# The attention sink of the windowed heads, as a column of the score tile

## What is computed

```
s_band = jnp.einsum('bnqhgd,bnkhd->bnhgqk', qb, kb).astype(F32) * scale
s_band = jnp.where(valid[None, :, None, None], s_band, -jnp.inf)
s_ctx = jnp.einsum('bnqhgd,bphd->bnhgqp', qb, k_ctx).astype(F32) * scale
s_sink = jnp.broadcast_to(sink.astype(F32).reshape(1, 1, Hk, G, 1, 1), s_band.shape[:-1] + (1,))
p = jax.nn.softmax(jnp.concatenate([s_band, s_ctx, s_sink], axis=-1), axis=-1)
p_band = p[..., :3 * BAND_BLOCK].astype(v.dtype)
p_ctx = p[..., 3 * BAND_BLOCK:3 * BAND_BLOCK + P].astype(v.dtype)
o = jnp.einsum('bnhgqk,bnkhd->bnqhgd', p_band, vb) + jnp.einsum('bnhgqp,bphd->bnqhgd', p_ctx, v_ctx)
```

## Time and profile before

| what | value |
|---|---|
| time, median of 3 runs | 1140.9 us (1140.78 to 1141.33) |
| the profiled execution | 1138.51 us, of which the span is 1136.7 us |
| TensorE busy | 1068.4 us, 94% of the span |
| VectorE busy | 416.9 us, 37% |
| ScalarE busy | 396.4 us, 35% |
| GpSimd busy | 538.1 us, 47% |
| mean granted TensorE clock | 0.979 of full |

### The profile page before, as it was taken

The page is one execution under the profiler, slowest core; times in us unless marked ns, Lnnn a source line. Parts: engine busy times, 40 slices in busy tenths (PEclk is TensorE's granted clock), DMA queues, the critical chain, the costliest instruction groups (busy, mean ns, idle before and its releaser), DMA issues.

```text
span 1136.7 us, 16312 instructions
## 1 busy us (share of the span) xinstructions
PE 1068.4 (94%) x6725; PEld 972.0 (86%) x6725; DVE 416.9 (37%) x850; ACT 396.4 (35%) x630; POOL 538.1 (47%) x422
## 2 busy tenths in 40 slices
PE   4799999997999999999999898789989999999997
PEld 3598899886989999999999696645879999999996
DVE  3757889157651111111112404286471111111222
ACT  0532332356343332232223423476334332332221
POOL 0364548541735555555557141230254566565662
PEclk9899999999989999999999998989989999999998
DMA  8633444546655666646668531620052454534441
GB/s 309 227 114 130 149 166 149 157 163 248 182 160 178 199 191 198 198 144 191 200 200 211 158 112 27 154 74 2 3 147 75 118 142 112 142 96 135 118 123 56
DMA packets 202053, 166.40 MB, mean 146 GB/s; under 512 B 20269, under 2 KB 184188, under 8 KB 201852
## 3 DMA queue, kind: packets, MB, share of 16 engines
q1 hardware_dynamic: 189280, 135.74, 40.2%
q10 hardware_dynamic: 12700, 29.63, 7.5%
HBM read 162.43 MB, written 2.92 MB: 145 GB/s over the span
## 4 chain that ended last, share of the span: by engine, by line
PE 83%; DVE 6%; ACT 3%; DMA 3%; POOL 2%; issue 1%; ACTq 0%; SPq 0%; DVEq 0%
PE banks L455 22%; PE banks L456 21%; PE banks L457 21%; PE banks L549 3%; PE banks L526 2%; PE banks L528 2%; PE banks L527 2%; POOL w_lo L1119 2%; PE banks L693 2%; DMA raw<-in_ada_w 2%; DVE ht L1621 1%; DVE h_lo L1612 1%; PE banks L542 1%; DMA xtok<-in_x_sample 1%; PE banks L990 1%
## 5 line engine op out<-in xcount | busy, mean ns | idle before, releaser
L1119 POOL TENSOR_TENSOR w_lo<-raw,w_hi 128x512 fp32r<-128x512 f32 (+2 forms) x398 | 512.7, 1319 | 581.4 <-ACT w_hi L1143 581.4
L455 PE MATMUL banks<-h_hi,w_hi 128*128 128x384 f32 (+1 forms) x1040 | 352.1, 339 | 6.0 <-DVE h_lo L1612 3.5
L457 PE MATMUL banks<-h_hi,w_lo 128*128 128x384 f32 (+1 forms) x1040 | 348.5, 335 | 0.0
L456 PE MATMUL banks<-h_lo,w_hi 128*128 128x384 f32 (+1 forms) x1040 | 348.4, 335 | 0.0
L1143 ACT ACTIVATE w_hi<-raw 128x2048 fp32r<-128x2048 f32 (+4 forms) x112 | 187.9, 1678 | 244.7 <-PE banks L457 135.8
L455 PEld LDWEIGHTS banks<-h_hi,w_hi 128*128 128x128 f32 (+1 forms) x1040 | 194.9, 187 | 16.0 <-issue 13.5
L456 PEld LDWEIGHTS banks<-h_lo,w_hi 128*128 128x128 f32 (+1 forms) x1040 | 195.1, 188 | 0.6
L457 PEld LDWEIGHTS banks<-h_hi,w_lo 128*128 128x128 f32 (+1 forms) x1040 | 195.0, 187 | 0.6
L1675 DVE TENSOR_TENSOR uf<-sa,banks 128x384 f32<-128x384 f32 x44 | 24.4, 554 | 325.1 <-PE banks L457 318.9
L455 PE MATMUL banks<-u_hi,w_hi 128*128 128x384 f32 x352 | 119.4, 339 | 0.0
L457 PE MATMUL banks<-u_hi,w_lo 128*128 128x384 f32 x352 | 118.2, 336 | 0.0
(11 more groups left out here) (324 smaller groups left out, 1184.3 us busy)
## 6 DMA issues: line engine op xcount, KB each, us to landing
raw<-in_ffn_w SPq DMA_DIRECT2D x88, 512.0 KB, 5.2
raw<-in_ada_w SPq DMA_DIRECT2D x28, 1024.0 KB, 6.3
raw<-in_ffn_w SPq DMA_DIRECT2D x32, 704.0 KB, 4.6
vada_raw<-in_ada_w ACTq DMA_DIRECT2D x20, 1024.0 KB, 6.5
raw<-in_w_in_even SPq DMA_DIRECT2D x18, 1024.0 KB, 5.3
raw<-in_w_out_even SPq DMA_DIRECT2D x4, 1024.0 KB, 6.2
raw<-in_w_in_odd SPq DMA_DIRECT2D x3, 1024.0 KB, 9.4
raw<-in_w_in_odd SPq DMA_DIRECT2D x8, 256.0 KB, 4.2
```

The lines of the kernel that those rows point to most:

```text
L455: pe.matmul(out, s_hi, m_hi, start=first and j == 0, stop=False)
L456: pe.matmul(out, s_hi, m_lo, start=False, stop=False)
L457: mm = pe.matmul(out, s_lo, m_hi, start=False, stop=last and j == len(terms) - 1)
L1119: ins = pool.tensor_tensor(low_part(s)[:, at:to], raw[u % RAW][:, at:to], high(s)[:, at:to].bitcast(F32), ALU.subtract)
```

## The change

The sink becomes one more key. `sink_score` holds sink times 8 (the inverse of the scale) on all partitions. `scores` writes it into a column behind each head's keys, with a matmul of the identity (stationary) and one column of `sink_score` (moving), in fp32. Maximum, exponential and row sum then run over 129 or 385 columns and take the sink in by themselves; the small steps L2022, L2024, L2035 and L1528 go, and sliding jobs take the one multiplication that low-rank jobs have. The scaling of the probabilities and the transposes leave the sink's column out. Because a head's probabilities take 385 columns, the halves of `pr` lie 386 apart instead of 384, and some tiles of the odd layer are laid out in another order, so that the larger `pr` finds room.

```diff
-        neg_sink = sb("neg_sink", [P, 8])
+        sink_score = sb("sink_score", [P, 8])
...
+        def width(job):
+            return job[5] + (job[0] == "swa")
...
                     for i, j in enumerate(pairs):
                         for x in range(2):
-                            mm = pe.matmul(both[:, 512 * x + i * nk:512 * x + i * nk + nk],
-                                           qc[64 * x:64 * x + 64, j, tq], kT[64 * x:64 * x + 64, k0:k0 + nk],
-                                           start=i == 0, stop=t == 0, skip_group_check=True)
+                            pe.matmul(both[:, 512 * x + i * wide:512 * x + i * wide + nk],
+                                      qc[64 * x:64 * x + 64, j, tq], kT[64 * x:64 * x + 64, k0:k0 + nk],
+                                      start=i == 0, stop=t == 0, skip_group_check=True)
+                    for i, j in enumerate(pairs):
+                        for x in range(2):
+                            at = 512 * x + i * wide + nk
+                            mm = pe.matmul(both[:, at:at + 1], ident, sink_score[:, 4 * x + j:4 * x + j + 1],
+                                           start=False, stop=True, skip_group_check=True)
...
-                            e = act.activation(pr_[:, 384 * x + i * nk:384 * x + (i + 1) * nk],
-                                               both[:, 512 * x + i * nk:512 * x + (i + 1) * nk], ACT.Exp,
+                            e = act.activation(pr_[:, SIDE * x + i * wide:SIDE * x + (i + 1) * wide],
+                                               both[:, 512 * x + i * wide:512 * x + (i + 1) * wide], ACT.Exp,
                                                scale=scale, bias=s_[:, 1, c:c + 1], accum_out=s_[:, 2, c:c + 1])
-                    if kind == "swa":
-                        e = act.activation(s_[:, 3, 0:nh], s_[:, 3, 0:nh], ACT.Exp)
...
-            step(dve.tensor_scalar(neg_sink[:, :], rowb[:, 0:8], -1.0, None, ALU.mult))
+            step(dve.tensor_scalar(sink_score[:, :], rowb[:, 0:8], 64 ** 0.5, None, ALU.mult))
...
-                    step(dve.tensor_reduce(two(0), sides(both[:, :], np_ * nk).rearrange("p x (i k) -> p x i k", i=np_),
+                    step(dve.tensor_reduce(two(0), sides(both[:, :], np_ * width(jobs[n])).rearrange("p x (i k) -> p x i k", i=np_),
                                            AX.X, ALU.max))
-                    if kind == "swa":
-                        step(dve.scalar_tensor_tensor(two(1), two(0), -scale, sinks(neg_sink[:, :], pairs),
-                                                      ALU.mult, ALU.min))
-                        dve.tensor_tensor(two(3), sinks(rowb[:, 0:8], pairs), two(1), ALU.add)\
-                            .then_inc(S["neg_max"], 1)
-                    else:
-                        dve.tensor_scalar(s_[:, 1, 0:nh], s_[:, 0, 0:nh], -scale, None, ALU.mult)\
-                            .then_inc(S["neg_max"], 1)
+                    dve.tensor_scalar(s_[:, 1, 0:nh], s_[:, 0, 0:nh], -scale, None, ALU.mult).then_inc(S["neg_max"], 1)
...
-                    if kind == "swa":
-                        step(dve.tensor_tensor(s_[:, 2, 0:nh], s_[:, 2, 0:nh], s_[:, 3, 0:nh], ALU.add))
                     step(dve.reciprocal(s_[:, 4, 0:nh], s_[:, 2, 0:nh]))
```

More of the change, by code:

```diff
@@ L132, in ada_units @@
     raise KeyError(place)
+SIDE = 386
 SEAM_UNITS = (("up0", 0), ("in1", 0), ("up1", 0))
@@ L252, in build @@
         PF, SI = PFSI[:, 0], PFSI[:, 1]
-        (const_odd, qc, kT, vt, cqf, ckvf, cq_hi, cq_lo, ckv_hi, ckv_lo, kr4, qn, qr, kn, vm, krr, rt, pr, pT,
-         cin_k, cin_c, cin_r, ident_r, band_r, out_k, out_c, out_r, st) = overlay([
-            ("const_odd", [P, NALL - NCONST], F32), ("qc", [P, 4, T], F32), ("kT", [P, TK], F32), ("vt", [P, 4, P], F32), ("cqf", [P, 3, T], F32),
+        (const_odd, ident_r, band_r, qc, kT, vt, cqf, ckvf, cq_hi, cq_lo, ckv_hi, ckv_lo, kr4, qn, qr, kn, vm, krr, rt,
+         cin_k, cin_c, cin_r, out_k, out_c, out_r, st, pT, pr) = overlay([
+            ("const_odd", [P, NALL - NCONST], F32), ("ident_r", [P, P], BF16), ("band_r", [P, 2, P], BF16),
+            ("qc", [P, 4, T], F32), ("kT", [P, TK], F32), ("vt", [P, 4, P], F32), ("cqf", [P, 3, T], F32),
             ("ckvf", [P, 2, T], F32), ("cq_hi", [P, 3, T], F32R), ("cq_lo", [P, 3, T], F32R),
@@ L259, in build @@
             ("qn", [P, 4, T], F32), ("qr", [P, 2, T], F32), ("kn", [P, 4, TK], F32), ("vm", [P, 4, 512], F32),
-            ("krr", [P, T], F32), ("rt", [P, 2, TL], F32), ("pr", [P, PR, 768], F32), ("pT", [P, 2, 768], F32),
+            ("krr", [P, T], F32), ("rt", [P, 2, TL], F32),
             ("cin_k", [P, P], F32), ("cin_c", [P, 256], F32), ("cin_r", [P, 4, 32], F32),
-            ("ident_r", [P, P], BF16), ("band_r", [P, 2, P], BF16),
-            ("out_k", [P, P], F32), ("out_c", [P, 256], F32), ("out_r", [P, 32], F32), ("st", [P, PR, 5, 4], F32)])
+            ("out_k", [P, P], F32), ("out_c", [P, 256], F32), ("out_r", [P, 32], F32), ("st", [P, PR, 5, 4], F32),
+            ("pT", [P, 2, 768], F32), ("pr", [P, PR, 2 * SIDE], F32)])
         _, x_hi, x_lo = overlay([("below", [P, 22848], F32), ("x_hi", [P, 2048], F32R), ("x_lo", [P, 2048], F32R)])
@@ L424, in sides @@
             return ap.rearrange("p (x n) -> p x n", x=2)[:, :, 0:w]
-        def sinks(ap, pairs):
-            return ap.rearrange("p (x j) -> p x j", x=2)[:, :, pairs[0]:pairs[-1] + 1]
+        def width(job):
+            return job[5] + (job[0] == "swa")
         vada_at_up = {f + 1: n // 4 for f, n in VADA_AT_UP.items() if n % 4 == 3}
@@ L949, in scores @@
                     pe.wait_ge(S["masks_ready"], 1)
-                both = score.fill(pe, ("s", n))
+                both, wide = score.fill(pe, ("s", n)), width(job)
                 tq = slice(t * P, (t + 1) * P)
@@ L985, in turned @@
                 both = turned_in.fill(pe, ("pT", n))
-                w = len(pairs) * nk
                 for x in range(2):
-                    for i in range(w // P):
-                        at = 384 * x + i * P
-                        tr = pe.transpose(both[:, 512 * x + i * P:512 * x + i * P + P], pr[:, n % PR, at:at + P], ident)
+                    for i in range(len(pairs)):
+                        for k in range(0, nk, P):
+                            at = SIDE * x + i * width(job) + k
+                            to = 512 * x + i * nk + k
+                            tr = pe.transpose(both[:, to:to + P], pr[:, n % PR, at:at + P], ident)
                 tr.then_inc(turned_in.done, 1)
@@ L1515, in _ @@
                     scale = 64 ** -0.5 if kind == "swa" else 96 ** -0.5
-                    s_, pr_, nh = st[:, n % PR], pr[:, n % PR], 2 * len(pairs)
+                    s_, pr_, wide = st[:, n % PR], pr[:, n % PR], width(jobs[n])
                     act.wait_ge(S["neg_max"], n + 1)
@@ L2039, in _ @@
                             c = x * np_ + i
-                            p = pr[:, (n - 1) % PR, 384 * x + i * nk:384 * x + (i + 1) * nk]
+                            at = SIDE * x + i * width(jobs[n - 1])
+                            p = pr[:, (n - 1) % PR, at:at + nk]
                             ins = dve.tensor_scalar(p, p, s_[:, 4, c:c + 1], None, ALU.mult)
```

## The result

The changed kernel takes 1143.3 us (median of 10 runs, 1140.85 to 1146.52), the kernel before, run beside it, 1140.2 us (10 runs, 1137.94 to 1142.05): a ratio of 1.0028 (95% interval 1.0017 to 1.004), 3.1 us slower. That lies in the range, near its upper end, and beyond the 0.2% up to which "the same" reached. The changed kernel's runs fall into two fives, 1140.9 to 1142.9 us at a mean granted clock of 0.976 or 0.977 and 1143.7 to 1146.5 us at one of 0.969 to 0.973, and the profiled execution (1141.55 us, span 1139.0, clock 0.976) is one of the first, so its trace shows less than the median loss.

What follows compares the result with a forecast made beforehand. The prediction took the sliding heads' stage as a ring of waits over TensorE, VectorE and ScalarE, its changes passed on one for one; +0.6+0.5-1.5+0.5 = +0.1 us on the 1140.9 median gave 1141.0 us, range 1138.3 to 1143.8.

Steps and rivals of the forecast that it cites:

- The first term: Start of the sliding heads' stage: job 0's sink instructions +0.89, removed VectorE step -0.19 and exponential -0.10, net +0.6 us.
- The second term: Half-clock stretch, about 738 to 744.5: eight sink instructions of jobs 2 and 3 cost 1.6, partly given back, +0.5 us.
- run there in half the time: Half-clock stretch: 2.2 us of work pushed past the clock's rise takes half as long there, 1.1 behind in all.
- The third term: GpSimd's two weight-split windows, 744.6 to 758.5: one caught VectorE step fewer in each, -1.5 us (ends -2.4 and +0.2).
- both scalings behind them were caught: GpSimd's windows: the normalising after the exponential is held up in both, giving back 2x1.3, so +0.2 us for this part.
- The fourth term: Steady part, four jobs: TensorE becomes the bound, turns of 3.19 against 3.05 us, +0.14x4, taken as +0.5 us.
- A: Ahead of job 2's scores: TensorE's gap shrinks to about 1.1 us, the clock does not fall; 1138.5 us, chance 0.17.
- B: Same stretch: a TensorE break before 744.5 prolongs half clock; 1144.3 us at worst, 1143.2 with one job hit, chance 0.18.
- in that stretch TensorE has a backlog: Half-clock stretch: argument against a break in TensorE's work before 744.5 that would keep the clock from rising.
- C: Sink instructions throughout the stage are nearly free, by the skill's issue-gap rule of about 25 ns; -2.2 us, 1138.7, chance 0.05.

## Why the prediction was off, step by step

**The first term held.** Fill: +0.6 forecast, +0.71 in the trace.

**The second term failed: the half-clock stretch, forecast at +0.5 us.** The price of a sink instruction in it was right (0.20 taken, 0.22 measured). Wrong was the step "run there in half the time", which kept the clock's return at 744.5, where it stood in the trace of before. It moved to 749.41, so nothing was given back. At job 4's start, where this part ends (744.69 before, 748.19 now), the changed kernel was 2.31 us behind, 0.71 of it from the fill: 1.6 us for this part, all of the 8x0.20, near the upper end of 1.7. A clock read from one execution was taken as fixed, while the change altered the very work ahead of it and under it.

**The third term's size held, by luck in part.** From job 4 to job 7 the changed kernel needs 11.39 us for 13.12: -1.7, where the sum had -1.5. One caught step took the place of two, as described, but both scalings behind them were caught, and that case the sum had priced at +0.2. The -1.7 is made of two larger numbers. Job 4's turn took 1.57 us more, with its scores at half clock and four sink instructions for which the sum has no term (the lag at job 5's start is 3.88). From job 5 to job 7 the changed kernel needs 6.85 us for 10.15, 3.3 less. The second half-clock stretch of the kernel before lay there (its value matmuls took 1.55 us for 0.88, job 6's scores 1.58 for 0.92); it is gone, and so is most of TensorE's waiting for VectorE. I read part of the 3.3 as no gain of the change by itself: TensorE, late by the half clock, lost time in which it had waited for VectorE before. The kernel with the steps off, which has no sinks and no such lag, wins 1.65 us from job 5 to job 7 (8.50 for 10.15), half of it. What is due to the steps and what to the missing half clock no run tells apart. In this execution the 3.3 give back what job 4 had lost and the second term, and the stage ends only 1.2 us late.

**The fourth term held in size, for another reason.** From job 7 to the low-rank heads it is 9.89 us for 9.30, +0.6 where +0.5 was forecast. TensorE became the bound, as forecast, but with turns of 2.99 us where 3.19 was taken and 3.05 stood before: -0.06 a turn, not +0.14 (four times 0.14 is 0.56, which the sum took as 0.5). What makes the part longer is its first turn, 3.92 us (759.58 to 763.50): GpSimd's second window now ends at 761.62 instead of 758.49 and reaches into it. The 2.74 for TensorE's turn without idle time was too much; without the sinks it is 2.53.

**The rivals.** A had the idle time right (1.1 forecast, 0.97 measured), but the clock fell all the same. B is what happened to that stretch; its own test (0.50 at 746) came out. Its reason did not: it asked for a break in TensorE's work before 744.5, and none opened after 739.91. Its price for one job hit, 1143.2, is within 0.1 us of the median measured, which is luck in part: the kernel before ran at 1140.2 beside it and not at 1140.9, so as a difference it is +2.3 against +3.1. The argument against it, "in that stretch TensorE has a backlog", was no protection. 0.18 was too little for it: no row of before showed one-column work at half clock, and the clock row of one execution was all that spoke for an early return. C fell for fp32: 0.12 us, not 0.025. For bf16 instructions the rule in the Trainium skill, "TensorE: Matmul & The Clock Gate", section "Back-to-back issue gap", holds (0.03 measured), so the sum should have asked what type the change needs.

In the traced execution the four parts come to +0.7, +1.6, -1.7 and +0.6, together +1.2 against +0.1: the miss there is the 1.1 us that were to be given back. The median's loss is 3.1 us, and the other 1.9 were not seen in a trace. Four of the changed kernel's ten runs have a mean granted clock of 0.969 to 0.972, below that of all 76 runs of the kernel before beside the experiments (0.973 to 0.984), and these are among its five longest. By the medians the clock makes 3.3 us of difference (+3.2 as it falls, -0.1 with fillers, uncertain by some 2.5), which is as much as the whole miss. So that the loss hangs on the clock is shown by the fillers; where the longer executions lose their further time is not. The range of the forecast held the median with nothing to spare: its upper end lies 2.9 us above the 1140.9 from which it was reckoned, and the kernel before ran 0.7 faster this time.

## What to carry to other kernels

Small matmuls that take the place of VectorE steps are priced by rows of the same stationary and the same type: with a full 128x128 stationary in fp32 each instruction held TensorE for 0.12 us (0.22 at half clock), in bf16 for 0.03, and that change of type alone turned 3 us lost into 4 us won. (The weight loads differ in the same sense, 192 and 96 ns, but that they set the spacing was not tested.) Where a stage has a stretch at half clock, a change that puts such work into it needs a range in which the stretch grows, and a copy with fillers is a cheap way to tell clock from work. If the two halves of a change can be run apart, do so: -3.0 and +7.9 told at once which estimate was bad.

## What the chip showed that was not expected

- The granted clock stayed at 0.50 over stretches in which TensorE was busy throughout: 12.0 of 12.0 us from 738 to 750 in the changed kernel with fillers behind job 1. The Trainium skill, "TensorE: Matmul & The Clock Gate", section "Part 1: The HAM clock gate", lets the clock rise after sustained work; a full queue as the trace counts it did not bring it here.
- Fillers in the wrong place do not help: with the same eight matmuls the kernel before lost its first fall, and the changed kernel had its longest (20.5 us).
- A wide VectorE step is caught by GpSimd as well as a small one: the scaling took 2.65 and 2.67 us for 0.75 where it started under GpSimd's instructions. Taking a small step away moved the catch to the wide one: VectorE lost 5.6 us so before and 5.9 in the changed kernel (sums over the two windows).
